# MLP up pieces by token tile, a first load in quarters, and weight chunks behind the last gather

## What is computed

```python
# first block, experts: 128 chosen rows for each token
h = gelu(einsum('td,ted->te', x, take(u, ids)))
out = einsum('te,ted->td', gates * h, take(v, ids))
# second block, each of four layers
x = x + attention_i(rms_norm(x, norm_mix[i]))
x = x + sqrelu_mlp(rms_norm(x, norm_mlp[i]), w_up[i], w_down[i])   # 1024 -> 4096 -> 1024
```

## Time and profile before

| | us |
|---|---|
| median of three runs | 2878.51 |
| the profiled execution, its own time | 2876.93 |
| its span, first to last instruction | 2875.1 |
| TensorE busy | 2528.3 (88%) |
| VectorE busy | 1749.2 (61%) |
| ScalarE busy | 963.4 (34%) |
| GpSimd busy | 641.0 (22%) |
| mean granted TensorE clock | 0.971 of full |

### The profile page before, as it was taken

One profiled execution on the slowest core, in us unless ns is written; L12 is line 12 of the kernel. 1 busy time (PEld: TensorE's weight loads), 2 busy tenths in 40 slices (PEclk: granted clock), 3 DMA queues, 4 the chain that ended last, 5 costly groups with the idle time before them and its releaser, 6 DMA issues.

```text
span 2875.1 us, 29037 instructions
## 1 busy us (share of the span) xinstructions
PE 2528.3 (88%) x9645; PEld 1559.3 (54%) x9645; DVE 1749.2 (61%) x3961; ACT 963.4 (34%) x2010; POOL 641.0 (22%) x625
## 2 busy tenths in 40 slices
PE   8888777799887899887877798999899889998999
PEld 3563222255452465432322356885588568865687
DVE  3557677756658666667776456554565556546655
ACT  1412122224222354222222234432444344424443
POOL 0014444433334333344444111002000000002000
PEclk9999999999999999999999999999999999999999
DMA  7139999999999999999999622544154315523352
GB/s 308 62 134 422 421 421 421 420 411 421 398 421 421 417 397 388 421 414 420 412 421 421 250 118 101 185 162 167 59 190 160 153 54 175 190 114 117 132 190 102
DMA packets 109904, 791.61 MB, mean 275 GB/s; under 512 B 12932, under 2 KB 15575, under 8 KB 18647
## 3 DMA queue, kind: packets, MB, share of 16 engines
q0 software_dynamic: 73760, 536.93, 45.3%
q1 hardware_dynamic: 36022, 253.21, 23.6%
HBM read 789.02 MB, written 1.07 MB: 275 GB/s over the span
## 4 chain that ended last, share of the span: by engine, by line
PE 62%; DMA 24%; DVE 7%; issue 3%; ACT 3%; POOL 1%; DVEq 0%; SPq 0%; ACTq 0%; POOLq 0%
DMA weights<-in_peer_uv,scratch 16%; PE psum L1201 13%; PE psum L1280 12%; PE psum L983 12%; PE psum L1264 9%; DMA arena<-in_peer_uv,scratch 8%; PE psum L1266 4%; PE psum L1056 2%; DVE heads_arena L2091 2%; PE psum L1064 2%; PE psum L967 1%; PE psum L1042 1%; PE psum L993 1%; PE psum L1031 1%; PE psum L1020 1%
## 5 line engine op out<-in xcount | busy, mean ns | idle before, releaser
L1201 PE MATMUL psum<-weights,scratch 128*128 128x512 f32 x1224 | 594.3, 625 | 163.9 <-ACT scratch L1579 163.9
L1201 PEld LDWEIGHTS psum<-weights,scratch 128*128 128x128 f32 x1224 | 231.9, 198 | 494.3 <-ACT scratch L1579 247.3
L1201 PE MATMUL psum<-arena,scratch 128*128 128x512 f32 x824 | 399.0, 619 | 88.9 <-ACT scratch L1579 88.9
L2546 POOL DMA_INDIRECT weights<-in_peer_uv,scratch x306 | 340.9, 1114 | 496.6 <-PE psum L1201 469.9
L2360 DVE TENSOR_TENSOR piece<-weights,piece 128x2048 fp32r<-128x2048 f32 x128 | 292.8, 2292 | 193.8 <-ACT piece L1672 193.8
L983 PE MATMUL psum<-weights,xT 128*128 128x512 f32 (+2 forms) x920 | 392.4, 583 | 15.6 <-DMA weights<-in_w_qkv_a 7.8
L1264 PE MATMUL psum<-split_x,piece 128*128 128x512 f32 x1024 | 371.8, 405 | 6.3 <-DVE split_x L2367 6.3
L1280 PE MATMUL psum<-piece,hidden 128*128 128x512 f32 x1536 | 358.8, 390 | 0.0
L1571 ACT ACTIVATE scratch<-scratch 128x2 f32<-128x2 f32 x256 | 52.0, 203 | 885.4 <-DVE heads_arena L2091 885.1
L2546 POOL DMA_INDIRECT arena<-in_peer_uv,scratch x206 | 234.2, 1137 | 461.9 <-PE psum L1201 328.8
L1201 PEld LDWEIGHTS psum<-arena,scratch 128*128 128x128 f32 x824 | 155.0, 196 | 306.9 <-issue 160.9
(11 more groups left out here) (224 smaller groups left out, 2656.6 us busy)
## 6 DMA issues: line engine op xcount, KB each, us to landing
weights<-in_w_up SPq DMA_DIRECT2D x64, 1024.0 KB, 4.9
weights<-in_w_down SPq DMA_DIRECT2D x64, 1024.0 KB, 4.9
weights<-in_w_kv_b SPq DMA_DIRECT2D x16, 1024.0 KB, 9.2
weights<-in_a_w_in SPq DMA_DIRECT2D x6, 2048.0 KB, 10.1
weights<-in_w_qkv_a SPq DMA_DIRECT2D x5, 2048.0 KB, 16.1
weights<-in_w_q_b SPq DMA_DIRECT2D x8, 1024.0 KB, 9.6
weights<-in_w_o_b SPq DMA_DIRECT2D x8, 1024.0 KB, 9.4
weights<-in_peer_w_q SPq DMA_DIRECT2D x8, 1024.0 KB, 9.8
```

Source lines behind the costliest of these rows:

```text
L1201: mm = pe.matmul(psum[g.bank][:, :], diagonal[:, n % DIAGONALS, :], row[:, D + half * BANK:D + (half + 1) * BANK], start=(k == 0), stop=(k ...
L2546: pool.indirect_dma_start(gathered[n % GATHER_SLOTS], None, rows, bass.IndirectOffsetOnAxis(ap=expert[:, w % NT, k:k + 1], axis=0), elemen ...
```

## The change

Three things change, on TensorE and SyncE alone.

1. The first two up pieces of each MLP. `up(0)` and `up(1)` become four calls: `up_first(0)`, tile 1's turn (moved here from before the MLP), `up_first(1)`, `up_second(0)`, `up_second(1)`. `up_first` has 16 matmuls of 256 columns, high weights by the high and low x of tile 0. `up_second` has 16 of the same for tile 1 and the 16 of L1266 for both tiles.
2. The first load is cut in four quarters of xT and of the chunk, each pair on one semaphore of its own; TensorE waits for one pair before every two blocks of its first group.
3. SyncE loads chunk 0 of layer 0's projection where it did, and then waits until the last gather has landed before it loads chunks 1 to 3.

```diff
@@ SyncE
-            lower, upper = slice(0, KB // 2), slice(KB // 2, KB)
-            sp.dma_start(xT[:, lower, :], A["x_turned"][:, lower, :]).then_inc(turned_loaded[0], 16)
-            sp.dma_start(first.view[:, lower, :], first.src[:, lower, :]).then_inc(first_loaded, 16)
-            sp.dma_start(xT[:, upper, :], A["x_turned"][:, upper, :]).then_inc(turned_loaded[1], 16)
-            sp.dma_start(first.view[:, upper, :], first.src[:, upper, :]).then_inc(weight_loaded[first.slot], 16)
+            for n in range(FIRST_PARTS):
+                part = slice(n * KB // FIRST_PARTS, (n + 1) * KB // FIRST_PARTS)
+                sp.dma_start(xT[:, part, :], A["x_turned"][:, part, :]).then_inc(first_loaded[n], 16)
+                sp.dma_start(first.view[:, part, :], first.src[:, part, :]).then_inc(first_loaded[n], 16)
...
             for l in layers:
-                load_weights(l.inp)
+                load_weights(l.inp, 0, 1)
+                if l.n == 0:
+                    last = WINDOWS * SEL - 1
+                    sp.wait_ge(gather_landed[last % GATHER_SLOTS], 16 * (last // GATHER_SLOTS + 1))
+                load_weights(l.inp, 1)
@@ TensorE, project
-                        if half_loaded and k == KB // 2:
-                            pe.wait_ge(turned_loaded[1], 16)
-                            pe.wait_ge(weight_loaded[c.slot], c.loaded)
+                        if in_parts and k % (KB // FIRST_PARTS) == 0:
+                            pe.wait_ge(first_loaded[k * FIRST_PARTS // KB], 32)
@@ TensorE, mlp
+                def up_first(n, q):
+                    piece_ready(q)
+                    w = m.piece("up", split_piece[q % SPLIT_SLOTS][0])
+                    for b, g in enumerate(m.up[n]):
+                        bank_free(g)
+                        for k in range(KB):
+                            if n == 0 and b == 0 and k % 4 == 0:
+                                pe.wait_ge(x_low.sem, m.x_low0 + 1 + k // 4)
+                            pe.matmul(halves_of(g, 0), w[:, k, b * P:(b + 1) * P], split_x_pair[:, k, :, 0:P], start=(k == 0), stop=False)
+
+                def up_second(n, q):
+                    w = [m.piece("up", part) for part in split_piece[q % SPLIT_SLOTS]]
+                    for b, g in enumerate(m.up[n]):
+                        for k in range(KB):
+                            if n == 0 and b == 0 and k % 4 == 0:
+                                pe.wait_ge(x_low.sem, m.x_low0 + 3 + k // 4)
+                            pe.matmul(halves_of(g, 1), w[0][:, k, b * P:(b + 1) * P], split_x_pair[:, k, :, P:T], start=False, stop=False)
+                            mm = pe.matmul(psum[g.bank][:, 0:T], w[1][:, k, b * P:(b + 1) * P], split_x[0][:, k, :],
+                                           start=False, stop=(k == KB - 1))
+                    mm.then_inc(piece_used.sem, 1)
+
+                def halves_of(g, t):
+                    return psum[g.bank][:, 0:2 * T].rearrange("p (a t) -> p a t", a=2)[:, :, t * P:(t + 1) * P]
...
-                up(0, 0)
-                up(1, 1)
+                up_first(0, 0)
+                turn_normed(l.mlp_turn[1], l.normed0 + 3)
+                up_first(1, 1)
+                up_second(0, 0)
+                up_second(1, 1)
                 four_pieces()
@@ TensorE, attend_tiles and the start
                 project(l.out_blocks[1][1:2])
-                turn_normed(l.mlp_turn[1], l.normed0 + 3)
-            pe.wait_ge(turned_loaded[0], 16)
-            pe.wait_ge(first_loaded, 16)
-            project(diff_qk_blocks[0:1], half_loaded=True)
+            project(diff_qk_blocks[0:1], in_parts=True)
```

More of the change, by code:

```diff
@@ L112 @@
 EARLY_SQUARES, EARLY_ROOT_IN, EARLY_NORM, EARLY_TURN, EARLY_CHUNK = 9, 10, 12, 14, 17
+FIRST_PARTS = 4
 SUBLN_STEPS, SUBLN_ROOT = (5, 7, 9, 12, 14, 16), 10
@@ L344, in build @@
         x_loaded = sem("x_loaded")
-        turned_loaded = [sem(f"turned_loaded{n}") for n in range(2)]
-        first_loaded = sem("first_loaded")
+        first_loaded = [sem(f"first_loaded{n}") for n in range(FIRST_PARTS)]
         consts_loaded = sem("consts_loaded")
@@ L648, in build @@
         diff_qk = TileProjection(diff_pieces[0:4], (0, 1, 2, 3), (0, 1, 2, 3, 4, 5, 6, 7))
+        slot_uses[0] -= 1
         diff_qk_blocks = [diff_qk.plan(t, n)[0] for n in range(4) for t in range(NT)]
@@ L968, in turns, with project @@
                     mm.then_inc(psum_filled[g.bank], 1)
-            def project(blocks, block0=0, turned=None, source=xT, half_loaded=False):
+            def project(blocks, block0=0, turned=None, source=xT, in_parts=False):
                 slot_chunk = None
                 for n, (c, c0, _, w, t, g) in enumerate(blocks):
-                    if c is not slot_chunk and not half_loaded:
+                    if c is not slot_chunk and c is not diff_qk.chunks[0]:
                         pe.wait_ge(weight_loaded[c.slot], c.loaded)
```

## The result

| | before | changed |
|---|---|---|
| median | 2882.33 us, 4 runs (2877.7 to 2887.59) | 2854.09 us, 4 runs (2849.25 to 2855.89) |
| ratio, 95% interval | | 0.9906 (0.9886 to 0.9925) |
| profiled execution, its span | 2876.93, 2875.1 | 2853.91, 2852.1 |
| TensorE busy | 2528.3 (88%) | 2529.7 (89%) |
| mean granted TensorE clock | 0.971 | 0.972 |

The changed kernel is 0.9% faster: 28.2 us, where 32.4 were forecast. The forecast of 2846 was 8 us too low, inside the range. TensorE's busy time is the same although the profiled span is 23 us shorter, so what went was waiting, and the mean clock says that the time at the lower level didn't go with it.

What follows compares the result with a forecast made beforehand. TensorE held 62% of the chain of waits and DMA 24%. MLP 24.7, start 1.8 and gathers 5.9 sum to 32.4 us off the profiled 2876.9, giving 2844.5; with 1.6 for the median, 2846, range 2839 to 2861.

Steps and rivals of the forecast that it cites:

- MLP, 24.7 predicted: Start of each MLP: the reordered up pieces save 24.7 us over four layers, 103.5 falling to 78.8.
- T: The end of the last output projection ahead of each MLP, from which the prediction counted its steps.
- the last term: In each MLP: `up(2)`, unchanged, takes 5.58 us, so the first down piece begins at T + 19.69.
- rival 2: MLP: weight loads bound narrow matmuls at 0.193 us, leaving 9.7 us saved in all, 2869 us; chance 0.05.
- rival 3: MLP: loads don't hide and the 1.2 GHz level stays, +16 us a layer, 2935 us in all; chance 0.03.
- about 17 us: MLP: the share of the 24.7 us that is work brought into idle time, the rest being the clock.
- rival 1: MLP: the clock still falls in each, losing 3.4 us a layer, 13.6 in all, 2860 us; chance 0.14.
- Quarters, 1.8 predicted: Start: waiting for 0.75 MB instead of 1.5 MB brings the first matmul to 6.0 instead of 7.82 us.
- The later quarters don't stall it: Start: two blocks last 3.4 us at the slow pace, longer than a quarter takes to land.
- Gathers, 5.9 predicted: End of the gathers: the last row lands 4.3 us earlier and the pair behind gains 1.6, 5.9 in all.
- 1.6 more: End of the gathers: with the clock kept, TensorE's pair behind the pause takes 3.43 us instead of 5.04.
- bound of 6.2: End of the gathers: the upper end of the predicted saving, whose lower end was 4.3 us.

Runs made afterwards that it cites:

- e6: The changed kernel with tile 1's turn ahead of all four up calls, so only the second idle time is filled: 2865.62 us.
- e7: The changed kernel with extra matmuls in idle times of the latent layer, at the selected keys' turn and ahead of each output turn: 2841.51 us.
- e1: The kernel before with the new order of the MLP alone: 2859.93 us, ratio 0.9918.
- e5: The changed kernel with only the first half of piece 0 ahead of tile 1's turn and piece 1 whole as it was: 2861.51 us.
- e8: The changed kernel with extra matmuls in idle times of the latent layer only: 2842.6 us, ratio 0.9872.
- second comparison: The changed kernel run once more, unaltered, against the kernel before: 2852.36 us, ratio 0.9907.
- e9: The changed kernel with extra matmuls at the selected keys' turn and ahead of each output turn, none in the latent layer: 2849.82 us.
- e10: e7 with three more extra matmuls ahead of the turn of tile 1's selected keys and one behind it: 2838.65 us, ratio 0.9851.
- e2: The kernel before with only SyncE's wait for the last gather ahead of chunks 1 to 3: 2872.48 us, ratio 0.9966.

## Why the prediction was right, and where it was off

**The bottleneck and the three places** were read rightly. Each part gives time where the prediction said, and the parts add up: alone they give 21.9, 9.4 and 0.3 us, 31.6 together, and the changed kernel stands 28 to 32 us below the kernel before in its two comparisons. Each of these gains is known to some 4 us either way, so that they add up is shown no more closely than that.

**MLP, 24.7 predicted, 22.8 measured** (102.5 to 79.7; 23.8 between the two first profiles). Step by step behind T: idle time ended at 3.50 (predicted 3.51), `up_first(1)` at 4.35 (4.39), `up_second` at 6.34 (6.43), `up(2)` at 14.10 (14.11), the first down piece at 19.91 (19.69). Only the last term was small by 0.2: an up piece takes 5.81 where the row of a busy stretch gave 5.58. The price of 0.12 for a narrow matmul holds to the hundredth, so rival 2 falls, and rival 3 with it. The Trainium skill (TensorE: Matmul & The Clock Gate, Back-to-back issue gap) would have given 0.109 by its formula for a single matmul's gap; the measured spacing of 0.12 decides. `up(2)` found its banks free without a wait. The split of the sum was wrong: "about 17 us" of work brought into idle time is 13.5, and the clock's share 9.3 instead of 7.7. Four times two fills of 1.92 less the added 0.3 is 14.2, which the prediction's own numbers would have said. Of the miss of 1.9 us the last term has 0.9; the other 1.0 is that one profile's 103.5 stood for all, where four give 102.5.

**Clock in the MLPs.** The forecast that it holds was right (1.00 in every window, eight transposes in 1.09), and rival 1 falls for these places. e6 shows what was at stake: with the pause whole the clock falls in all four layers.

**Quarters, 1.8 predicted, 1.4 measured** (0.8 in the first profile). The mis-sized term is the first landing: 6.43 and not 6.0, so 0.75 MB less is worth 1.4 us at the head of the program and not what the gathers' steady pace gives. "The later quarters don't stall it" holds at the slow pace but for 0.17 us once in e7. Where the clock happened to rise early they did, as in e7's weight loads:

```profile
10.99 0.48 PEld L988 LDWEIGHTS psum<-weights,xT 128*128 128x128 f32 x2 [0.38 <-DMA weights<-in_w_qkv_a]
...
12.94 0.30 PEld L988 LDWEIGHTS psum<-weights,xT 128*128 128x128 f32 x2 [0.61 <-DMA weights<-in_w_qkv_a]
```

TensorE shows no later wait for constants or the second chunk, which were costed at nothing.

**Gathers, 5.9 predicted, 5.5 in the first profile, 7.0 on average.** The distance of the last dot products (2.46), the idle time (1.22) and the following pair (3.53, 3.43 forecast) are near what was predicted, and chunk 1 isn't waited for. The mis-sized term is what the pair behind the late landing loses, "1.6 more". It took 5.04 us in the one profile that the prediction read, and 6.1 to 6.4 in the other four without the wait, where more of it ran at the lower clock; so on average 2.5 us are lost there. With 4.4 us less idle time (1.2 instead of 5.6 on average) that is nearly all of the 7.0. The bound of 6.2 was too tight for that reason. The second profile of the kernel before shows such a pair:

```profile
1623.22 6.59 PE L1201 MATMUL psum<-weights,scratch 128*128 128x512 f32 x8 [5.66 <-ACT scratch L1579]
1629.65 3.60 PE L1201 MATMUL psum<-arena,scratch 128*128 128x512 f32 x8
```

**What the sum left out.** The prediction asked whether the clock falls in the new stretch and never what a kept clock does behind it. Every term ended at the first down piece, and all that follows was taken to move along unchanged. It doesn't: layer 2 takes 6.6 us more (285.0 on average in the changed kernel and e1, against 278.5 in the four with the old order), layer 1 2.2 us more (277.9 against 275.7); layer 3 is 2.9 shorter (288.9 against 291.8) and the stretch ahead of the first MLP 1.0 longer (123.8 against 122.7), both within what single profiles of one kind differ by. Layer 1's 2.2 is doubtful too, since e5, e6 and e8, which have no extra matmuls in layer 1, show 275.4 to 276.3.

Together these are 6.9 us, which leaves 24.3 of the three parts' 31.2; the two profiles of each kernel differ by 22.3 on average. The medians differ by more, and they split the 8.1 us between 2846 and 2854.1 in another way: 4.2 are a smaller gain (28.2 instead of 32.4), and 3.8 are that the kernel before was itself slower than the 2878.5 that was started from. In the second comparison (31.8) the gain is nearly the forecast one. So the loss in layer 2 is shown for the profiled executions, and the account by places and the medians can't be joined more closely than some 4 us.

What happens in layer 2 is rival 1 in kind, a fall of the clock that eats part of the gain, but at a place that none of the rivals named. Before the change the prediction could have seen the place: the same pauses are in the trace of the kernel before. In both kernels the clock is low over the transposes (0.60 in the changed kernel's window from 2276 to 2280 us); in the changed one it is low a second time over the attention. What decides on that second fall isn't settled. That the MLP before it fixes how the following layers lie against the clock's switching would fit, e6 included, but was only argued.

**The comparison of the one profile with the median.** The prediction set the median 1.6 us above the profiled execution, from three runs. In the 46 timed runs beside the experiments the kernel before goes from 2869.95 to 2887.72, and the time follows the mean granted clock: 2869.95 at 0.976, 2887.72 at 0.963. Its two profiled executions (2876.93, 2874.58) are both from the faster half (the median of the 46 is 2880.7). So the profiles differ by 23 us where the medians differ by 28, and what the slower executions of the kernel before lose beyond that stands in neither profile.

## What to carry to other kernels

When a change closes a pause of the engine whose clock is gated, price the pauses behind it as well: list every idle time ahead of dense work in the profile with the granted clock of the windows that follow, since time won at one may be lost at the next. A few unneeded matmuls into a free bank, placed in the pause and shorter than it, are a cheap test of what the clock costs (2.3 us an MLP here) and can be kept as a fix (10.9 us for this kernel, side by side). A bulk load that nobody needs yet should be kept behind the last transfer that somebody waits for.

## What the runs showed of the hardware

- A 128x256 fp32r matmul with new weights each time goes at 0.12 us at full clock, 80 in a row (9.75 us from 1760.49 to 1770.24), though the row of its weight load shows 0.193.
- The clock's rise at the start came 3.4 to 6.6 us behind the first matmul in 14 profiles of two kinds of start, and some of its falls lie elsewhere in two executions of the same kernel. The Trainium skill (TensorE: Matmul & The Clock Gate, Part 1: The HAM clock gate) says that the window of the activity monitor is free-running and doesn't reset when a kernel starts. The spread of the kernel before, 2870 to 2888 at clocks of 0.976 to 0.963, and the moving rise at the start are consistent with that. With pauses filled the spread was 2.5 us in e7, 1.8 in e9, 7.3 in e10 and 13.8 in e8, of four runs each: too few to say that it is narrower.
- Small matmuls fed without idle time stayed at 0.50 in the changed kernel's layer 2 with TensorE busy for 4.00 of 4 us by its rows (the window from 2288 us), and the same work stayed at 1.00 where it began at 1.00 (e8).
- One load of 2 MB behind a gather of 1 MB made its landing 4.3 us late (6.76 us behind the one before, in rows 5, instead of 2.46). It was issued at 1612.55, a second one at 1619.22, 3 us before the gather was there; from 1616 to 1620 us the gathers' queue moved 4 packets and the loads' queue 95. The Trainium skill (DMA: Bandwidth & Descriptors, Queues, rings and completion order) says that an engine takes turns between the queues that have work; that both queues move packets in that stretch, and that e2 alone brings the landing back to the pace, agree. Why so few of the packets are the gather's isn't shown.
